# Moving the last conditioning sum of a projection behind the first weight item of the next one, and cutting a known-root input ahead of the first item's low parts

## The reference

```python
# first block
x = x + 0.5 * _swiglu(_rmsnorm(x, ffn1_norm), ffn1_w_gu, ffn1_w_down)
h = _rmsnorm(x, mix_norm)
u_hy, u_rw, g_hy, g_rw = jnp.split(h @ w_in, split_at, axis=-1)
...
x = x + merged @ w_out
x = x + 0.5 * _swiglu(_rmsnorm(x, ffn2_norm), ffn2_w_gu, ffn2_w_down)
# second block, two layers l
ada = cond @ ada_w[l] + ada_b[l]                 # cond = silu(c), one row; 6 * 1024 columns
h = modulate(rmsnorm(x, norm_g[l, 0]), sh1, sc1)
...                                              # layer 0: mLSTM mixer, layer 1: MLA attention
kv_shift, kv_scale = jnp.split(cond @ kv_ada_w + kv_ada_b, 2, axis=-1)
...
x = x + g1[:, None, :] * rmsnorm(y, norm_g[l, 1])
h = modulate(rmsnorm(x, norm_g[l, 2]), sh2, sc2)
y = sqrelu_mlp(h, mlp_w1[l], mlp_w2[l])          # square(relu(h @ w1)) @ w2
x = x + g2[:, None, :] * rmsnorm(y, norm_g[l, 3])
```

## Time and profile before

| | |
|---|---|
| time, median of 3 runs | 3241.93 us (3240.22 to 3247.28) |
| the profiled execution: its own time / its span | 3243.93 us / 3242.1 us |
| PE matmuls | 2813.5 us busy, 87% of the span, 17297 |
| PE weight loads | 2199.6 us, 68% |
| DVE | 1592.8 us, 49% |
| ACT | 873.1 us, 27% |
| POOL | 400.5 us, 12% |
| mean granted TensorE clock | 0.916 |
| transfers | 272.78 MB, mean 84 GB/s |

### The profile page before, as it was taken

One profiled execution on the slowest core, in us unless ns is written; L12 is line 12 of the kernel. 1 busy time (PEld: TensorE's weight loads), 2 busy tenths in 40 slices (PEclk: granted clock), 3 DMA queues, 4 the chain that ended last, 5 costly groups with the idle time before them and its releaser, 6 DMA issues. The chain is left out here.

```text
span 3242.1 us, 40247 instructions
## 1 busy us (share of the span) xinstructions
PE 2813.5 (87%) x17297; PEld 2199.6 (68%) x17297; DVE 1592.8 (49%) x2116; ACT 873.1 (27%) x1114; POOL 400.5 (12%) x376
## 2 busy tenths in 40 slices
PE   7999997788587769999998979589999659889998
PEld 5887874777462458788876853368877446668886
DVE  5554456666655453565545224644263535353342
ACT  3221234111134112322213233332221333432221
POOL 1111001111001110111100001212030100021010
PEclk8999998899798789999998987789999779989999
DMA  5554530000020022355543310123243210223231
GB/s 159 160 159 153 163 100 21 3 3 3 28 73 26 0 65 85 98 162 168 167 141 123 100 34 2 52 65 107 95 137 121 53 44 2 78 67 103 91 104 52
DMA packets 267299, 272.78 MB, mean 84 GB/s; under 512 B 10559, under 2 KB 248102, under 8 KB 266927
## 3 DMA queue, kind: packets, MB, share of 16 engines
q1 hardware_dynamic: 251760, 208.32, 21.0%
q0 software_dynamic: 15360, 61.87, 5.8%
HBM read 268.07 MB, written 2.10 MB: 83 GB/s over the span
## 5 line engine op out<-in xcount | busy, mean ns | idle before, releaser
L836 DVE TENSOR_TENSOR mlp_wl<-mlp_raw,mlp_wh 128x2048 fp32r<-128x2048 f32 x74 | 189.9, 2566 | 290.7 <-ACT mlp_wh L732 290.7
L836 DVE TENSOR_TENSOR mix_wl<-mix_raw,mix_wh 128x2048 fp32r<-128x2048 f32 (+2 forms) x66 | 153.1, 2320 | 244.6 <-ACT mix_wh L732 244.5
L658 PE MATMUL mix_ps<-h_mix_hi,mix_wh 128*128 128x512 f32 x624 | 245.1, 393 | 9.2 <-ACT mix_wh L732 9.2
L660 PE MATMUL mix_ps<-h_mix_lo,mix_wh 128*128 128x512 f32 x624 | 243.7, 390 | 0.0
L732 ACT ACTIVATE mix_wh<-mix_raw 128x2048 fp32r<-128x2048 f32 (+2 forms) x66 | 117.6, 1781 | 246.0 <-PE mix_ps L664 162.1
L732 ACT ACTIVATE mlp_wh<-mlp_raw 128x2048 fp32r<-128x2048 f32 x74 | 140.5, 1899 | 154.0 <-PE mlp_ps L664 88.8
L658 PE MATMUL ffn_ps<-h_rw_hi,ffn_wh 128*128 128x512 f32 x448 | 175.2, 391 | 0.0
L660 PE MATMUL ffn_ps<-h_rw_lo,ffn_wh 128*128 128x512 f32 x448 | 174.3, 389 | 0.0
L664 PE MATMUL mix_ps<-h_mix_hi,mix_wl 128*128 128x512 f32 x624 | 154.2, 389 | 0.0
L658 PE MATMUL mlp_ps<-view,mlp_wh 128*128 128x512 f32 x384 | 150.1, 391 | 0.0
L660 PE MATMUL mlp_ps<-view,mlp_wh 128*128 128x512 f32 x384 | 149.5, 389 | 0.0
(11 more groups left out here) (560 smaller groups left out, 6111.5 us busy)
## 6 DMA issues: line engine op xcount, KB each, us to landing
mlp_raw<-in_mlp_w SPq DMA_DIRECT2D x64, 1024.0 KB, 5.3
ffn_sraw<-in_ada_w POOLq DMA_DIRECT2D x34, 768.0 KB, 5.3
ffn_raw<-in_ffn_w_gu SPq DMA_DIRECT2D x44, 512.0 KB, 5.2
mix_raw<-in_ffn_w_gu SPq DMA_DIRECT2D x44, 512.0 KB, 4.6
mix_sraw<-in_ada_w POOLq DMA_DIRECT2D x22, 768.0 KB, 5.2
mix_raw<-in_a_w_in SPq DMA_DIRECT2D x12, 1024.0 KB, 5.3
mix_sraw<-in_kv_ada_w POOLq DMA_DIRECT2D x12, 768.0 KB, 4.9
ffn_raw<-in_w_in SPq DMA_DIRECT2D x8, 1024.0 KB, 5.3
```

The source lines that it names most:

```text
L658: nc.tensor.matmul(ps[:, it.banks[t], :], w(h, k, t), xh[:, k, :], start=it.first and k == it.k0, stop=False)
L660: nc.tensor.matmul(ps[:, it.banks[t], :], w(h, k, t), xl[:, k, :], start=False, stop=False)
L836: nc.vector.tensor_tensor(slot(wl, it), slot(raw, it), slot(wh, it).bitcast(F32), ALU.subtract)\
```

## The change

It has two parts.

**The last sum is owed.** `side_sums` for the last pair of items is not issued at the end of its projection but noted in `owed`, and issued after `products` of the first item of the next projection. Norms between the two projections are passed over. DVE does the same with `side_take`: it comes at the first item of the next projection, behind `take_out` and `lower` of that item and ahead of that projection's own `side_half`.

**The first item.** For item 0 of a `dense` call, where it is fresh, PE no longer waits for `wl` ahead of everything: it makes all products of weight high by input high, then waits, then makes those of weight low by input high, and then the rest as before. This concerns `ffn1`, `hy_in`, `mlp0` and `mlp1`; in `mix` the first item is not fresh. Where the first step is a norm with a known root (`hy_in` alone), ACT makes the high part of the first four input slices, then `upper` of item 0, then the other four; DVE makes the eight pieces of the input and then `lower` of item 0. Before, both took item 0 first.

```diff
--- before.py
+++ after.py
@@ -637,13 +637,20 @@
                 elif it.fresh:
                     for t in ts:
                         bank_free(it, t)
-                    pe.wait_ge(lo_ready, it.n + 1)
+                    if it.n > 0:
+                        pe.wait_ge(lo_ready, it.n + 1)
                     for k in ks:
                         wait_hi(pe, st.parts, k)
                         for t in ts:
                             nc.tensor.matmul(ps[:, it.banks[t], :], w(h, k, t), xh[:, k, :],
                                              start=it.first and k == it.k0, stop=False)
-                            nc.tensor.matmul(ps[:, it.banks[t], :], w(l, k, t), xh[:, k, :], start=False, stop=False)
+                            if it.n > 0:
+                                nc.tensor.matmul(ps[:, it.banks[t], :], w(l, k, t), xh[:, k, :], start=False, stop=False)
+                    if it.n == 0:
+                        pe.wait_ge(lo_ready, 1)
+                        for k in ks:
+                            for t in ts:
+                                nc.tensor.matmul(ps[:, it.banks[t], :], w(l, k, t), xh[:, k, :], start=False, stop=False)
                     for k in ks:
                         wait_lo(pe, st.parts, k)
                         for t in ts:
@@ -698,11 +705,15 @@
                                             start=True, stop=True)
                 last.then_inc(side_sum, 1)
 
+            owed = None
             for st in steps:
                 if isinstance(st, Gemm):
                     fed = st.feeds if isinstance(st.feeds, Norm) else None
                     for i, it in enumerate(st.items):
                         products(it)
+                        if owed and i == 0:
+                            side_sums(owed, len(owed.items) // 2 - 1)
+                            owed = None
                         if fed and i > 0 and st.items[i - 1].last:
                             for j in st.items[i - 1].js:
                                 sum_tile(fed, j)
@@ -712,12 +723,14 @@
                         for j in st.items[-1].js:
                             sum_tile(fed, j)
                     if st.side:
-                        side_sums(st, len(st.items) // 2 - 1)
+                        owed = st
                 elif isinstance(st, Norm) and not st.known:
                     if st.fed is None:
                         for k in range(st.n):
                             sum_tile(st, k)
                     spread_root(st)
+            if owed:
+                side_sums(owed, len(owed.items) // 2 - 1)
 
         @block.scalar
         def _(act):
@@ -810,11 +823,13 @@
                     if started == 0:
                         upper(items[0])
                     root(st)
-                elif started == 0:
+                elif started == 0 and not isinstance(st, Norm):
                     upper(items[0])
                 if st.kind == "parts" and (isinstance(st, Norm) or st.fed is None):
                     for k in range(st.n):
                         first_part(st, k)
+                        if started == 0 and isinstance(st, Norm) and st.known and k == st.n // 2 - 1:
+                            upper(items[0])
                 if isinstance(st, Norm) and st.root is not None and not st.known:
                     act.wait_ge(pieces, st.piece[-1])
                     nc.scalar.activation(st.root, rs[:, :], ACT.Copy).then_inc(saved, 1)
@@ -957,7 +972,7 @@
                         nc.vector.scalar_tensor_tensor(out[:, k, :], st.src[:, k, :], gk, by, ALU.mult, ALU.mult)\
                             .then_inc(pieces, 1)
 
-            started = 0
+            started, owed = 0, None
             if isinstance(steps[0], Gemm):
                 lower(items[0])
                 lower(items[1])
@@ -969,15 +984,21 @@
                             take_out(it)
                         if following(it) and not late(it):
                             lower(following(it))
+                        if owed and i == 0:
+                            side_take(owed)
+                            owed = None
                         if st.side:
                             side_half(st, i)
                     if st.side:
-                        side_take(st)
+                        owed = st
                     continue
-                if started == 0:
+                known = isinstance(st, Norm) and st.known
+                if started == 0 and not known:
                     lower(items[0])
                 if isinstance(st, Norm):
                     pieces_of(st)
+                if started == 0 and known:
+                    lower(items[0])
                 if st.kind == "parts":
                     for k in range(st.n):
                         if not st.on_pool[k]:
```

## The result

The changed kernel takes 3196.66 us in the median of four runs (3191.8 to 3203.16). The kernel before, run beside it on the same chip, takes 3241.41 us. The ratio is 0.986, with a 95% interval of 0.9838 to 0.9881: 44.8 us less, where 39.1 were forecast.

A forecast was written before the change was run, and what follows sets the result against it. PE was taken as the bound within projections, with time to win where it stands still or runs at the lower clock. Terms 31.3 - 4.1 + 4.6 + 3.6 + 3.7 = 39.1 us took 3241.93 to 3202.8 us, range 3195 to 3216.

The forecast's parts named there:

- The handovers: Up to down projection in `ffn1`, `mix`, `mlp0`: PE's wait and the slow products after it vanish, 31.3 us gained.
- The side sums: Six last side sums, now between two items of a PE-bound projection, cost 0.68 us each: -4.1 us.
- The norms: Three norms behind down projections: DVE's reciprocal starts earlier without `side_take` ahead of it, 4.6 us gained.
- The first items: PE starts before the low weight: 3.6 us at `mlp0` and `mlp1` together, 3.7 at `hy_in`, 0 in `ffn1`.
- The clock: Restarts after pauses throughout the kernel may have more or fewer slow matmuls, adding up at random: 5 us either way.
- The pushed-back stall: Rival: PE stalls an item later in the down projection, losing about 5 us per handover: 3218 us, chance 0.14.
- The starved first items: Rival: PE waits for ACT in `mlp0`, `mlp1`, `ffn1`, `hy_in` first items, giving back 6.8 us: 3210, chance 0.10.
- The side weights' stream: Rival: shifted side transfers land late, DVE holds back `lower`, and PE is paced by it: slower than before, chance 0.03.

The follow-up runs named there:

- owed_only: The kernel before with only the owed sums, first items prepared and multiplied as before: 3206.15 us, ratio 0.9885.
- handover_only: The kernel before with sums owed only where up hands over to down; ahead of a norm they are taken at once: 3207.64 us, ratio 0.9895.
- known_only: The kernel before with only `hy_in`'s preparation order on ACT and DVE changed; PE still waits for the low weight first: 3237.04 us, single run.
- cut_first: The changed kernel with input parts made ahead of item 0's weight parts on ACT and DVE in calls beginning with a `Cut`: 3197.06 us, ratio 0.9867.
- after_again: The changed kernel, unaltered, run and traced a second time, against the kernel before: 3196.27 us, ratio 0.9862.

## Why the prediction was right

**The handovers (31.3 us).** Right in mechanism and size. The waits are gone, the clock in the windows is 1.00, and the next product comes after 1.81 us; the three stretches are 31.3 us shorter. `owed_only` gains 10.7 us in `ffn1`, 11.8 in `mix` and 10.3 in `mlp0`, 32.8 in all, where the handovers, the sums in their new place and the norms were to give 31.8; its median is 34.0 us lower. Its profiled execution, the fastest of the four (3201.26 us; the others 3206.04 to 3206.48), has the heads' 5.8 and the scan's 4.2 us on top. That the first down item needs nothing late was the step on which all hung, and the earlier trace rows had shown it.

**The side sums (-4.1 us).** The row carried: 0.68 us at the place that I read, 0.68 or 0.69 at the other three places with six matmuls and 0.46 at `mlp0`'s two with four, 3.7 us in all. Read as a price of any number of such matmuls it would have been wrong, as the run with five times as many shows.

**The norms (4.6 us).** The reciprocals are 1.40 and 2.02 us earlier against the start of the last side operations, for 1.33 and 1.94 forecast, and 1.3 in `mlp0`. So the wait was read rightly. What the term left out is the clock behind it: the first product comes 6.0 us earlier at the three norms together, and the 32 products behind it take 2.7 us longer than in `handover_only`. After the sums, 1.5 us of the 2.5 reach the ends of the three calls.

**The first items (3.6 and 3.7 us).** `hy_in` gained 3.9 us for 3.7, and `known_only` splits it. From `upper` to PE, `mlp0` and `mlp1` gained 1.76 us each for 1.8; their starts gained 1.3 to 1.4 and 1.8 to 1.9, as the weights landed. But the text counted starts only. The `mlp0` call gained 9.1 us where 10.3 were due (464.7 us without the first-item edit, 465.9 with it), and the 0.7 us of it that the first item's rows show come from more products at the lower clock. The term of 3.6 us is the one most mis-sized: less what `mlp0` gives back, it was worth about 2 in these traces. That `mlp1`'s call grew by 1.4 us as well I can't put down to the edit: its first 32 products are not slower, and it is 421.7 us in `cut_first`, which has the edit too. In `ffn1` nothing starves: the changed kernel's call is as long as that of `owed_only` to 0.2 us.

**The clock (5 us either way).** The sum over the edited stages was 1.5 to 1.9 us below the forecast gain, the median 6.1 below the predicted time. The first trace, of the slowest of the four runs, lies 1.6 us below its own forecast of 3204.8, because 7.0 us lost in the long convolutions cancel most of the scan's 4.2 and the heads' 5.8. The trace of `after_again` lies at the median: there 10.5 us came from untouched stages. No term of the sum stands for those 10.5 us, and they bring the median to 1.7 us above the lower edge of the range; that they were not more is luck. The spread named the clock and was slightly too small for it. One point was argued too simply: I thought of many restarts of about 1 us each that add up at random. Three stages carry most of it: over all traces the scan goes from 260.6 to 267.4 us, the heads from 95.0 to 104.6, and the long convolutions from 207.0 to 218.6.

**The rivals.** The pushed-back stall did not appear: PE has no wait for a low weight in the first down items, and the windows show it busy. The starved first items did not appear: PE takes no wait for ACT inside a first item, and what `mlp0` gives back, 1.2 us instead of 6.8 for all, goes with the clock as far as the rows show it. The side weights' stream did not stall anything.

## What to carry to other kernels

A helper product that must wait for another engine belongs behind the first chunk of the next large one, not between the two: it costs 0.5 to 0.7 us there, and between them it cost 10 us here with the slow products that follow a pause. Before moving it, look in the trace for the same handover without it; that row says whether another wait is hidden behind. And when small gains are summed, compare stage by stage: here 3 to 10 us of the difference between two traces lay in stages with identical instructions. An earlier restart should also be followed to the end of its stage: part of what the norms and `mlp0` gained at the first product was gone 32 products later.

## What was unexpected in the hardware

- A stage with 5790 small matmuls and unchanged instructions took 267.3, 263.1 or 260.6 us, at a granted clock of 0.93, 0.97 or 0.99. Seven cleared tiles ahead of it (4.5 us), or two (1.8 us), shortened it by 6.7 us in the kernel before; seven shortened it by nothing in `cut_first`.
- The mLSTM heads took 95.1, 100.9 or 104.6 us at a clock of 0.85, 0.80 or 0.77. What selects among them is open.
- The same products behind the same pause (`mix`, behind the norm) took 10.22 and 8.72 us in two executions of one kernel.
- Thirty one-column matmuls in a row, 4.29 us in which PE is shown busy, are followed by products at a mean clock of 0.64 for 6.6 us. Six in a row are not.
